# mLSTM: half of all heads' score weights made inside the projection, then the heads in pairs in the same block

## The chip, the cores and the metric

The kernel runs on one core of one Trainium2 chip. The metric is the device time of one execution in microseconds (us); where several runs are shown, their median.

## The reference, cut to what matters

One sequence of 256 tokens with 1024 features passes through three blocks of layers. The change touches one mixer of the third block, the mLSTM: 8 heads, queries and keys of 64, values of 128. Per head it computes, with `b` the running sum of the log forget gate and `li` the input gate:

```
qk = silu(causal_conv(proj[..., :2*M_QK]))
d  = where(mask, b[t] - b[s] + li[s], NEG)
m_t = maximum(inter, max(d))
s  = einsum(q, k) * exp(d - m_t)
den = sum(s)
h  = s @ v / maximum(abs(den), exp(-m_t))
out = (head_rmsnorm(h) * sigmoid(o)) @ w_out
```

The reference does this in chunks of 64 tokens with a carried state; the kernel does it for all 256 tokens at once, where no state is left.

## The kernel before, in words

The whole network is one program. A stage is a `nc.Block()`: inside it each engine runs its own list of instructions, in order, and at its end all engines meet. Weights stream from memory as chunks of 2 MB or 1.5 MB into a ring of four (`ring`); the queue of SyncE asks for the next as the tensor engine lets one go.

A product with exact float32 result is made of three products of rounded halves. The scalar engine writes the rounded part of a quarter of a chunk (`weights.high`, line 339, `weight_hi`), the vector engine the remainder (`weights.low`, line 346, `weight_lo`), and the tensor engine multiplies high by high, high by low and low by high (lines 516 to 518). A quarter of a chunk is called a part below. There are four places for parts. The scalar engine may write part b once the tensor engine has begun part b - 3, and the tensor engine may begin part b once the vector engine has done its remainder. So a part that is ready waits for up to three parts of tensor work.

The mLSTM mixer is `mlstm` (line 2589), in two stages:

- **Projection** (line 2600). Two chunks give queries and keys (parts 0 to 7), with one small product for the gates between them. Each block of 128 channels goes through the convolution on the vector engine (lines 2691, 2693) and Silu on the scalar engine (2665). Four more chunks give the values `v` (parts 8 to 15) and the output gate `out_gate` (parts 16 to 23). After the first of these the tensor engine turns the running sum into `decay` and repeats the key gates over all partitions (line 2635), and the scalar engine copies them to `key_gate` (2671). The vector engine copies each finished chunk product out of the banks (2708). At the end Sigmoid is applied to the whole `out_gate` (2675).
- **Heads** (line 2724). The loop at line 2737 takes one head after another. The lower triangle of 256 by 256 is kept as 384 columns: 128 for the first half of the queries ("near") and 256 for the second ("far"). Per head: the vector engine adds key gate, decay and mask (2773), takes the maximum of each row (2777) and turns it into a bias (2779, 2780); the scalar engine takes the exponential (2807); the vector engine multiplies by the scores of the tensor engine (2743, 2744) and sums (2788), makes the divisor (2792 to 2794) and scales the rows (2796); the tensor engine turns the three 128 by 128 pieces (2751), the scalar engine copies them to `weight_t` (2814), and the tensor engine multiplies by the values (2759 to 2761). `weight` and `weight_t` have two places each, and the order in which each engine goes through the steps of heads i, i-1 and i-2 is written out by hand.

The next stage is `add_gated`. It begins with the norm of each head (`HeadNorm`, line 2560 squares, 2568 sums, 2580 on GpSimd weighs the gate), turns the result (line 538) and multiplies it by `w_out`.

Of the kernel before, what the change touches and what calls it, by code (L numbers as in the profile page):

```python
# [22 lines left out]
ALU = mybir.AluOpType  # L23
ACT = mybir.ActivationFunctionType
# [347 lines left out]
def build(nc, d, widths, offsets):  # L372
    ctx = ExitStack()
    with ctx:
# [2214 lines left out]
        def mlstm(mem, x_parts, normalise):  # L2589
# [10 lines left out]
            with ExitStack() as conv, signals(  # L2600
                    "params_loaded", "t_ready", "t_read", "n_ready", "n_read", "dve_step", "pad_ready", "convolved", "o_copied",
                    "act_step", "summed", "turned", "pool_step", "pick_ready", "repeated", "repeated_read", *PARTS, *PreNorm.SIGNALS) as (
                    params_loaded, t_ready, t_read, n_ready, n_read, dve_step, pad_ready, convolved, o_copied,
                    act_step, summed, turned, pool_step, pick_ready, repeated, repeated_read, *sems):
                weights = weight_parts("t.tnnnn", sems[:len(PARTS)], conv)
                norm = normalise(x_parts, sems[len(PARTS):], conv, out_gate)
                raw = sbuf("raw", [P, DK, before + TOKENS], mem=conv)
                block = conv.enter_context(nc.Block())
# [31 lines left out]

                @block.scalar
                def _(act):
# [19 lines left out]
                    for b in range(DK):  # L2662
                        weights.high(act, DK + 4 + b // 3)
                        act.wait_ge(convolved, b + 1)
                        act.activation(qkT[:, b, :], qkT[:, b, :], ACT.Silu, bias=col("conv_b", b))
# [3 lines left out]
                    for n in range(HEADS_C // 2):  # L2669
                        act.wait_ge(repeated, n + 1)  # L2670
                        act.activation(key_gate[:, 2 * n:2 * n + 2, :], ps[:, (3, 0, 1, 3)[n], :].rearrange("p (b n) -> p b n", b=2),
                                       ACT.Copy).then_inc(repeated_read, 1)
                    weights.high(act, 24)
                    act.wait_ge(o_copied, 2)
                    act.activation(out_gate[:], out_gate[:], ACT.Sigmoid)

                @block.vector
                def _(dve):
# [25 lines left out]
                    for n in range(4):  # L2704
                        out = v if n < 2 else out_gate
                        weights.low(dve, DK + 4 * n + 7)
                        dve.wait_ge(n_ready, n + 1)
                        dve.tensor_copy(out[:, :, n % 2 * WIDE:n % 2 * WIDE + WIDE], bank_n(n)).then_inc(n_read, 1)
                        if n >= 2:
                            dve.wait_ge(n_read, n + 1)  # L2710
                            dve.memset(spare[:], 0.0).then_inc(o_copied, 1)
# [7 lines left out]

            with signals("scored", "biased", "exped", "probs_ready", "probs_turned", "turned_copied", "weighted", "dve_step") as (
                    scored, biased, exped, probs_ready, probs_turned, turned_copied, weighted, dve_step), ExitStack() as att:
                weight = sbuf("weight", [P, 2, TRI], mem=att)
                weight_t = sbuf("weight_t", [P, 2, TRI], mem=att)
                top = sbuf("top", [P, 2, TT], mem=att)
                least = sbuf("least", [P, 2, TT], mem=att)
                total = sbuf("total", [P, 2, TT], mem=att)
                part = (slice(0, P), slice(P, TRI))  # L2730
                keys = (P, TOKENS)
                n = HEADS_C
                block = att.enter_context(nc.Block())

                @block.tensor
                def _(pe):
                    for i in range(n + 2):
                        if i < n:
                            half = slice(i % 2 * HD, i % 2 * HD + HD)
                            if i >= 2:  # L2740
                                pe.wait_ge(probs_ready, i - 1)
                            q, k = qkT[half, i // 2, :], qkT[half, 4 + i // 2, :]
                            pe.matmul(ps[:, i % 2, 0:P], q[:, 0:P], k[:, 0:P], start=True, stop=True)
                            pe.matmul(ps[:, i % 2, P:TRI], q[:, P:TOKENS], k, start=True, stop=True).then_inc(scored, 1)
                        j = i - 1
                        if 0 <= j < n:
                            pe.wait_ge(probs_ready, j + 1)
                            if j >= 2:
                                pe.wait_ge(turned_copied, j - 1)
                            for b in range(3):  # L2750
                                last = pe.transpose(ps[:, 2 + j % 2, b * P:b * P + P], weight[:, j % 2, b * P:b * P + P], ident[:])
                            last.then_inc(probs_turned, 1)
                        j = i - 2
                        if j >= 0:
                            pe.wait_ge(turned_copied, j + 1)
                            t = weight_t[:, j % 2, :]
                            out = [ps[:, 4 + 2 * (j // 4) + a, j % 4 * P:j % 4 * P + P] for a in range(TT)]
                            val = [v[:, s, j * P:j * P + P] for s in range(TT)]
                            pe.matmul(out[0], t[:, 0:P], val[0], start=True, stop=True, skip_group_check=True)
# [827 lines left out]
```

## Time and profile before

| | |
|---|---|
| median of 3 runs | 3304.74 us (3301.76 to 3308.48) |
| profiled execution | 3303.2 us |
| its span, first to last instruction | 3301.5 us |
| mean granted clock of the tensor engine | 0.944 |
| tensor engine busy | 2961.6 us (90%) |
| vector engine busy | 2160.7 us (65%) |
| scalar engine busy | 1558.0 us (47%) |
| GpSimd busy | 104.1 us (3%) |

The tensor engine is busy in 90% of the span, but not evenly: the page's row of 40 slices has single slices at 5 tenths. The busy share of matmuls is of modelled ends, so a busy tensor engine isn't one at its peak. The granted clock is a share of full speed: 1.00 is 2.4 GHz, 0.50 is 1.2 GHz. Times in a timeline are from the start of the span.

### The profile page before, as it was taken

How to read it: one execution, taken by the hardware profiler on the slowest of the kernel's cores; microseconds unless marked ns; L12 is line 12 of the kernel's file. 1: busy time of each engine (PE TensorE's matmuls, PEld its weight loads, DVE VectorE, ACT ScalarE, POOL GpSimd, SP SyncE). 2: the span in 40 equal slices, each digit the busy share in tenths (PEclk: the TensorE clock that was granted, in tenths of full speed). 3: DMA queues.
4: the chain of work that ended last, by engine and by line, in shares of the span. 5: the costliest groups of instructions: out<-in, count | busy, mean ns of one | idle time of the engine just before them, and what ended most of it. 6: DMA issues, size and time to landing. Idle time of an engine off the chain costs nothing. (4 is left out here: it accounts for less than half of the span.)

```text
span 3301.5 us, 48307 instructions
## 1 busy us (share of the span) xinstructions
PE 2961.6 (90%) x19343; PEld 2611.4 (79%) x19343; DVE 2160.7 (65%) x3342; ACT 1558.0 (47%) x2451; POOL 104.1 (3%) x131
## 2 busy tenths in 40 slices
PE   7897998899999997778989799978997579999997
PEld 6896876579999997657977698758986569999996
DVE  5456598666666665276655665665555858888887
ACT  3442313444444444164443544534344248787875
POOL 0000000000000000200000000000000200000000
PEclk9998999999999998899998899969999879999999
DMA  6343498755666553304442254413553038888895
GB/s 270 145 179 139 160 369 344 307 198 203 217 209 223 193 199 142 124 26 153 178 163 106 102 181 151 167 50 134 191 188 113 0 150 334 338 332 325 330 336 189
DMA packets 76828, 648.61 MB, mean 196 GB/s; under 512 B 6105, under 2 KB 31193, under 8 KB 34033
## 3 DMA queue, kind: packets, MB, share of 16 engines
q1 hardware_dynamic: 49584, 621.09, 50.4%
q10 hardware_dynamic: 27072, 25.17, 2.3%
q8 instruction: 116, 1.90, 0.2%
q14 instruction: 56, 0.45, 0.0%
HBM read 632.60 MB, written 13.63 MB: 196 GB/s over the span
## 5 line engine op out<-in xcount | busy, mean ns | idle before, releaser
L1190 PE MATMUL ps<-x_hi,up_hi 128*128 128x256 f32 x1632 | 460.5, 282 | 3.7 <-DVE up_lo L1281 3.5
L346 DVE TENSOR_TENSOR weight_lo<-ring,weight_hi 128x1024 fp32r<-128x1024 f32 x236 | 288.4, 1235 | 263.5 <-ACT weight_hi L339 255.4
L1193 PE MATMUL ps<-x_lo,up_hi 128*128 128x256 f32 x1632 | 459.6, 282 | 0.0
L1194 PE MATMUL ps<-x_hi,up_lo 128*128 128x256 f32 x1632 | 459.5, 282 | 0.0
L339 ACT ACTIVATE weight_hi<-ring 128x1024 fp32r<-128x1024 f32 x236 | 245.7, 1054 | 190.6 <-PE ps L516 124.8
L1286 DVE TENSOR_TENSOR down_lo<-ring,down_hi 128x1024 fp32r<-128x1024 f32 x182 | 222.9, 1224 | 165.9 <-ACT down_hi L1243 165.9
L1190 PEld LDWEIGHTS ps<-x_hi,up_hi 128*128 128x128 f32 x1632 | 311.1, 191 | 11.8 <-DVE up_lo L1281 4.1
L1193 PEld LDWEIGHTS ps<-x_lo,up_hi 128*128 128x128 f32 x1632 | 311.1, 191 | 6.7
L1194 PEld LDWEIGHTS ps<-x_hi,up_lo 128*128 128x128 f32 x1632 | 311.1, 191 | 0.0
L1243 ACT ACTIVATE down_hi<-ring 128x1024 fp32r<-128x1024 f32 x182 | 193.2, 1062 | 232.1 <-PE ps L1215 232.1
L494 PE MATMUL ps<-x_hi,weight_hi 128*128 128x256 f32 x1024 | 291.5, 285 | 8.9 <-DVE weight_lo L346 8.1
L3283 DVE TENSOR_TENSOR up_lo<-ring,up_hi 128x1024 fp32r<-128x1024 f32 x242 | 294.4, 1217 | 4.2 <-ACT up_hi L3402 4.2
L495 PE MATMUL ps<-x_lo,weight_hi 128*128 128x256 f32 x1024 | 289.1, 282 | 0.0
L496 PE MATMUL ps<-x_hi,weight_lo 128*128 128x256 f32 x1024 | 288.9, 282 | 0.0
L3200 PE MATMUL ps<-up_hi,taken_hi 128*128 128x256 f32 x968 | 285.7, 295 | 2.1 <-DVE seat L3287 2.1
L1211 PE MATMUL ps<-down_lo,hidden_hi 128*128 128x512 f32 x728 | 285.7, 392 | 0.0
L1207 PE MATMUL ps<-down_hi,hidden_hi 128*128 128x512 f32 x728 | 284.1, 390 | 0.0
L3202 PE MATMUL ps<-up_hi,taken_lo 128*128 128x256 f32 x968 | 274.4, 283 | 0.0
L3201 PE MATMUL ps<-up_lo,taken_hi 128*128 128x256 f32 x968 | 274.2, 283 | 0.0
L3402 ACT ACTIVATE up_hi<-ring 128x1024 fp32r<-128x1024 f32 x242 | 256.1, 1060 | 32.5 <-PE ps L3202 25.0
L1281 DVE TENSOR_TENSOR up_lo<-ring,up_hi 128x1024 fp32r<-128x1024 f32 (+1 forms) x182 | 245.4, 1349 | 16.8 <-ACT up_hi L1237 16.8
L1215 PE MATMUL ps<-down_hi,hidden_lo 128*128 128x512 f32 x728 | 224.8, 390 | 0.0
(508 smaller groups left out, 6368.0 us busy)
## 6 DMA issues: line engine op xcount, KB each, us to landing
ring<-in_stream SPq DMA_DIRECT2D x181, 2048.0 KB, 7.8
ring<-in_experts SPq DMA_DIRECT2D x121, 1536.0 KB, 8.5
ring<-in_stream SPq DMA_DIRECT2D x22, 1536.0 KB, 6.4
gates<-kept_gates ACTq DMA_DIRECT2D x12, 1024.0 KB, 8.8
kept_gates<-away_first ACTq DMA_DIRECT2D x8, 768.0 KB, 10.6
kept_gates<-away_last ACTq DMA_DIRECT2D x8, 768.0 KB, 9.3
params_mix<-in_mix SPq DMA_DIRECT2D x1, 3072.0 KB, 21.9
params_ln<-in_ln SPq DMA_DIRECT2D x2, 1024.0 KB, 5.3
```

What stands on the lines that cost most here:

```text
L346: dve.tensor_tensor(self.place(self.lo, b), self.raw(b), self.place(self.hi, b), ALU.subtract).then_inc(self.split, 1)
L494: first = pe.matmul(out, hi[:, k, :], x_parts[0][:, k, :], start=(k == 0), stop=False)
L495: second = pe.matmul(out, hi[:, k, :], x_parts[1][:, k, :], start=False, stop=False)
L496: last = pe.matmul(out, lo[:, k, :], x_parts[0][:, k, :], start=False, stop=(k == DK - 1))
L1190: last = pe.matmul(out, hi[:, o:o + P], x_hi[:, k, :], start=(k == 0), stop=False)
L1193: pe.matmul(out, hi[:, o:o + P], x_lo[:, k, :], start=False, stop=False)
L1194: last = pe.matmul(out, lo[:, o:o + P], x_hi[:, k, :], start=False, stop=(k == DK - 1))
L1207: last = pe.matmul(out, hidden_hi[:, j % 2, tokens], hi[:, o:o + WIDE], start=(starts and i is None and j == 0), stop=False, skip_group_ch ...
L1211: pe.matmul(out, hidden_hi[:, j % 2, tokens], lo[:, o:o + WIDE], start=False, stop=False, skip_group_check=True)
L3200: pe.matmul(to, taken_hi[:, s % 3, k, :], hi, start=(k == 0), stop=False, skip_group_check=True)
L3202: last = pe.matmul(to, taken_lo[:, s % 3, k, :], hi, start=False, stop=(k == DK - 1), skip_group_check=True)
L3283: dve.tensor_tensor(up_part(up_lo, g, half), raw_up(g, half), up_part(up_hi, g, half), ALU.subtract).then_inc(up_split, 1)
```

## The change

The second stage of the mLSTM is gone; its work moves into the projection's stage.

- The vector engine makes the biased triangle, the row maxima and the biases of heads 0 to 3 between the remainders of parts 15 to 18, ahead of the copy of chunk product 1, and those of heads 4 to 7 between the remainders of parts 19 to 22, ahead of the copy of product 2. The steps on the maxima are made once for four heads.
- The scalar engine takes the exponentials of four heads after each of these, with parts 19 and 23 of the weights in between.
- All eight heads' triangles are kept, in the buffers `hT` (heads 0 to 4) and `raw` (heads 5 to 7), which are free by then; `weight_t`, `top`, `least` and `total` lie in the rest of `raw`.
- After the last projection matmul the heads go in pairs. The divisor is made once for two heads, and the scaling of the far columns moves from the vector engine to the scalar engine.
- The Sigmoid on `out_gate` is made in two halves, after the copies of pair 0 and of pair 1.

The diff, cut:

```diff
+                    def scores(p):
+                        for h in (2 * p, 2 * p + 1):
...
+                            pe.matmul(ps[:, h % 2, 0:P], q[:, 0:P], k[:, 0:P], start=True, stop=True)
+                            pe.matmul(ps[:, h % 2, P:TRI], q[:, P:TOKENS], k, start=True, stop=True).then_inc(scored, 1)
...
+                    pe.wait_ge(qk_ready, DK)
+                    pe.wait_ge(repeated_read, n_pairs)
+                    scores(0)
+                    pe.wait_ge(n_read, 4)
+                    for p in range(n_pairs):
+                        if p + 1 < n_pairs:
+                            pe.wait_ge(multiplied, p + 1)
+                            scores(p + 1)
+                        if p >= 1:
+                            values(p - 1)
+                        for h in (2 * p, 2 * p + 1):
+                            pe.wait_ge(near_ready, h + 1)
+                            pe.wait_ge(far_ready, h + 1)
+                            for b in range(3):
+                                last = pe.transpose(ps[:, 2 + h % 2, b * P:b * P + P], probs[h][:, b * P:b * P + P], ident[:])
+                            last.then_inc(probs_turned, 1)
+                    values(n_pairs - 1)
```

```diff
                 @block.scalar
+                    for g, heads in enumerate(halves):
+                        weights.high(act, DK + 11 + 4 * g)
+                        act.wait_ge(biased, g + 1)
+                        act.activation(least[:, heads[0]:heads[-1] + 1, :], top[:, heads[0]:heads[-1] + 1, :], ACT.Exp)
+                        for h in heads:
+                            for t in range(TT):
+                                o = probs[h][:, part[t]]
+                                last = act.activation(o, o, ACT.Exp, bias=top[:, h, t:t + 1])
+                            if h % 2 == 1:
+                                last.then_inc(exped, 1)
+                                weights.high(act, DK + 12 + 4 * g if h == heads[1] else 0)
                     weights.high(act, 24)
-                    act.wait_ge(o_copied, 2)
-                    act.activation(out_gate[:], out_gate[:], ACT.Sigmoid)
+                    for p in range(n_pairs):
+                        act.wait_ge(divided, p + 1)
+                        for h in (2 * p, 2 * p + 1):
+                            o = probs[h][:, part[1]]
+                            act.activation(o, o, ACT.Copy, scale=total[:, h, 1:2]).then_inc(far_ready, 1)
+                        for h in (2 * p, 2 * p + 1):
+                            act.wait_ge(probs_turned, h + 1)
...
+                            act.activation(weight_t[h % 2], ps[:, 2 + h % 2, 0:TRI], ACT.Copy).then_inc(turned_copied, 1)
+                        if p < TT:
+                            act.wait_ge(n_read, 4)
+                            act.activation(out_gate[:, p, :], out_gate[:, p, :], ACT.Sigmoid)
```

```diff
                 @block.vector
                     for n in range(4):
+                        if n in (1, 2):
+                            heads = halves[n - 1]
...
+                            dve.tensor_scalar(top[:, some, :], top[:, some, :], -1.0, None, ALU.mult).then_inc(biased, 1)
                         weights.low(dve, DK + 4 * n + 7)
                         dve.wait_ge(n_ready, n + 1)
                         dve.tensor_copy(out[:, :, n % 2 * WIDE:n % 2 * WIDE + WIDE], bank_n(n)).then_inc(n_read, 1)
-                        if n >= 2:
-                            dve.wait_ge(n_read, n + 1)
-                            dve.memset(spare[:], 0.0).then_inc(o_copied, 1)
+                    for p in range(n_pairs):
+                        dve.wait_ge(exped, p + 1)
+                        s = total[:, 2 * p:2 * p + 2, :]
+                        for h in (2 * p, 2 * p + 1):
+                            dve.wait_ge(scored, h + 1)
+                            for t in range(TT):
+                                o = probs[h][:, part[t]]
+                                last = dve.scalar_tensor_tensor(o, o, HD ** -0.5, ps[:, h % 2, part[t]], ALU.mult, ALU.mult,
+                                                                accum_out=total[:, h, t:t + 1])
+                        last.then_inc(multiplied, 1)
...
+                        dve.reciprocal(s, s).then_inc(divided, 1)
+                        dve.wait_ge(divided, p + 1)
+                        for h in (2 * p, 2 * p + 1):
+                            o = probs[h][:, part[0]]
+                            dve.tensor_scalar(o, o, total[:, h, 0:1], None, ALU.mult).then_inc(near_ready, 1)
```

The vector engine in the projection, before, from the copy of chunk product 0 to that of product 2:

```order
L2708 COPY v<-ps 128x2x512
L346 TENSOR_TENSOR weight_lo<-ring,weight_hi 128x1024 x4
L2708 COPY v<-ps 128x2x512
L346 TENSOR_TENSOR weight_lo<-ring,weight_hi 128x1024 x4
L2708 COPY out_gate<-ps 128x2x512
```

and with the change, from the copy of product 0 to that of product 1:

```order
L2802 COPY v<-ps 128x2x512
L346 TENSOR_TENSOR weight_lo<-ring,weight_hi 128x1024
L2789 SCALAR_TENSOR_TENSOR hT<-key_gate,decay,mask 128x128
L2789 SCALAR_TENSOR_TENSOR hT<-key_gate,decay,mask 128x256
...
L346 TENSOR_TENSOR weight_lo<-ring,weight_hi 128x1024
L2795 TENSOR_REDUCE raw<-hT 128x1 x8
L346 TENSOR_TENSOR weight_lo<-ring,weight_hi 128x1024
L2798 TENSOR_TENSOR raw<-raw,decay 128x8
L2799 TENSOR_SCALAR raw<-raw 128x8
L2802 COPY v<-ps 128x2x512
```

Where four remainders stood alone, eight additions (L2789), eight maxima and two small steps stand between them and ahead of the copy; the group between products 1 and 2 has the same form.

The scalar engine after the last exponential of the projection, with the change:

```order
L2742 ACTIVATE hT<-hT,raw 128x256 x2
L2747 ACTIVATE raw<-ps 128x384 x2
L2750 ACT_TABLE_LOAD
L2750 ACTIVATE out_gate<-out_gate 128x1024
L2742 ACTIVATE hT<-hT,raw 128x256 x2
L2747 ACTIVATE raw<-ps 128x384 x2
L2750 ACTIVATE out_gate<-out_gate 128x1024
```

L2742 is the scaling of the far columns, L2747 the copy of the turned pieces, L2750 the Sigmoid. Before, the Sigmoid stood ahead of the whole second stage; now its table load and first half stand between pair 0 and the far columns of pair 1, its second half between pairs 1 and 2.

The tensor engine, with the change, from the first scores to the turning of pair 1:

```order
L2662 MATMUL ps<-qkT 128x128
L2663 MATMUL ps<-qkT 128x256
...
L2690 MATMUL ps<-ident,hT 128x128 x6
L2662 MATMUL ps<-qkT 128x128
L2663 MATMUL ps<-qkT 128x256
L2662 MATMUL ps<-qkT 128x128
L2663 MATMUL ps<-qkT 128x256
L2671 MATMUL ps<-v,raw 128x128
L2672 MATMUL ps<-v,raw 128x128
L2673 MATMUL ps<-v,raw 128x128
...
L2690 MATMUL ps<-ident,hT 128x128 x6
```

L2662 and L2663 are scores, L2671 to L2673 values, L2690 turns a pair's six pieces. Two heads' scores now stand next to each other, and the scores of the next pair and the values of the pair before stand ahead of each turning.

## Rows read from the trace of the kernel before

**Rows 1.** Busy time of each engine by stretch: projection, change of stage, heads

```profile
core 0: us, PE busy (x) PEld busy (x) DVE busy (x) ACT busy (x) POOL busy (x), PEclk, DMA share, GB/s
2117.00:2156.00 39.00, 39.00 (x163) 31.32 (x162) 14.74 (x13) 13.40 (x15) 0.00 (x0) 0.96 0.37 140
2156.00:2160.00 4.00, 0.37 (x4) 0.11 (x2) 1.35 (x3) 2.03 (x2) 0.00 (x0) 0.81 0.00 0
2160.00:2190.00 30.00, 21.29 (x77) 15.51 (x77) 22.42 (x100) 10.37 (x28) 0.00 (x0) 0.50 0.00 1
```

**Rows 2.** Waits in the heads' stage: who waited for whom, us in total, times, longest

```profile
PE ps L2751 <- DVE weight L2796: 9.5, 7, 3.6
ACT least L2804 <- DVE top L2780: 9.4, 8, 1.3
```

**Rows 3.** Timeline of the vector engine, one head: start, us, engine, line, operation

```profile
2179.71 0.75 DVE L2773 SCALAR_TENSOR_TENSOR weight<-key_gate,decay,mask 128x128 f32<-128x128 f32 x2 [0.99 <-PE ps L2751]
2180.49 0.61 DVE L2777 TENSOR_REDUCE top<-weight 128x1 f32<-128x128 f32 x2
...
2181.42 0.29 DVE L2788 SCALAR_TENSOR_TENSOR weight<-weight,ps 128x128 f32<-128x128 f32 x1
...
2182.09 0.16 DVE L2792 SCALAR_TENSOR_TENSOR total<-total 128x2 f32<-128x2 f32 x1
...
2182.68 0.55 DVE L2796 TENSOR_SCALAR weight<-weight,total 128x128 f32<-128x128 f32 x2
```

**Rows 4.** Timeline of the scalar engine: a table load, the Sigmoid, one head

```profile
2105.15 1.28 ACT L2661 ACT_TABLE_LOAD   x1
2106.45 0.42 ACT L2661 ACTIVATE gate_t<-gate_t 8x256 f32<-8x256 f32 x1
...
2157.72 1.91 ACT L2675 ACTIVATE out_gate<-out_gate 128x2048 f32<-128x2048 f32 x1 [9.98 <-DVE spare L2711]
...
2181.65 0.78 ACT L2807 ACTIVATE weight<-weight,top 128x128 f32<-128x128 f32 x2
...
2184.23 0.49 ACT L2814 ACTIVATE weight_t<-ps 128x384 f32<-128x384 f32 x1 [1.80 <-PE ps L2751]
```

**Rows 5.** Timeline of the tensor engine: last projection matmul, heads 0 and 1, head 5, the end

```profile
2155.90 0.39 PE L518 MATMUL ps<-weight_hi,x_lo 128*128 128x512 f32 x1
...
2159.92 0.81 PE L2743 MATMUL ps<-qkT 64*128 64x128 f32 x4 [3.63 <-PEq L2600]
2160.48 1.10 PE L2744 MATMUL ps<-qkT 64*128 64x256 f32 x4
...
2183.29 0.91 PE L2751 MATMUL ps<-ident,weight 128*128 128x128 f32 x3 [0.76 <-DVE weight L2796]
2183.99 0.64 PE L2759 MATMUL ps<-v,weight_t 128*128 128x128 f32 x2
...
2185.41 0.79 PE L2743 MATMUL ps<-qkT 64*128 64x128 f32 x2
...
2196.57 0.39 PE L2761 MATMUL ps<-v,weight_t 128*128 128x128 f32 x2
```

**Rows 6.** Timeline of the vector engine: copies of chunk products, the last remainder

```profile
2133.94 1.23 DVE L2708 COPY v<-ps 128x1024 f32<-128x1024 f32 x1 [0.25 <-PE ps L518]
...
2146.46 1.23 DVE L346 TENSOR_TENSOR weight_lo<-ring,weight_hi 128x1024 fp32r<-128x1024 f32 x1
...
2156.33 1.23 DVE L2708 COPY out_gate<-ps 128x1024 f32<-128x1024 f32 x1 [8.64 <-PE ps L518]
```

**Rows 7.** The scalar engine's roundings in the projection's last 39 us, with mean ns

```profile
L339 ACT ACTIVATE weight_hi<-ring 128x1024 fp32r<-128x1024 f32 x9 | 9.6, 1061 | 15.3 <-PE ps L516 15.2
```

**Rows 8.** Busy time by stretch in another mixer's heads (columns as in rows 1)

```profile
1434.80:1458.80 24.00, 19.52 (x162) 12.32 (x164) 23.25 (x52) 19.47 (x68) 0.00 (x0) 1.00 0.00 1
1462.20:1469.00 6.80, 3.76 (x32) 2.52 (x34) 3.36 (x10) 4.06 (x11) 0.00 (x0) 1.00 0.02 4
```

**Rows 9.** The tensor engine's transposes there

```profile
L1070 PE MATMUL ps<-ident,prob 128*128 128x128 f32 x48 | 7.0, 282 | 4.9 <-DVE prob L1094 4.9
```

More of the change, by code:

```diff
@@ L2607, in mlstm @@
                 raw = sbuf("raw", [P, DK, before + TOKENS], mem=conv)
+                hT_flat = hT[:].rearrange("p k n -> p (k n)")
+                raw_flat = raw[:].rearrange("p k n -> p (k n)")
+                in_hT = DK * TOKENS // TRI
+                probs = [hT_flat[:, h * TRI:h * TRI + TRI] if h < in_hT else raw_flat[:, (h - in_hT) * TRI:(h - in_hT) * TRI + TRI]
+                         for h in range(HEADS_C)]
+                raw_rest = raw_flat[:, (HEADS_C - in_hT) * TRI:]
+                weight_t = [raw_rest[:, b * TRI:b * TRI + TRI] for b in range(2)]
+                top, least, total = (raw_rest[:, 2 * TRI + b * HEADS_C * TT:2 * TRI + (b + 1) * HEADS_C * TT].rearrange("p (h t) -> p h t", t=TT)
+                                     for b in range(3))
+                part = (slice(0, P), slice(P, TRI))
+                keys = (P, TOKENS)
+                halves = (range(0, HEADS_C // 2), range(HEADS_C // 2, HEADS_C))
+                n_pairs = HEADS_C // 2
                 block = conv.enter_context(nc.Block())
@@ L2664, in _ @@
                         act.wait_ge(convolved, b + 1)
-                        act.activation(qkT[:, b, :], qkT[:, b, :], ACT.Silu, bias=col("conv_b", b))
+                        act.activation(qkT[:, b, :], qkT[:, b, :], ACT.Silu, bias=col("conv_b", b)).then_inc(qk_ready, 1)
                     weights.high(act, DK + 7)
@@ L2705, in _ @@
                         out = v if n < 2 else out_gate
+                        if n in (1, 2):
+                            heads = halves[n - 1]
+                            some = slice(heads[0], heads[-1] + 1)
+                            for h in heads:
+                                if h % 2 == 0:
+                                    weights.low(dve, DK + 4 * n + 4 + h % 4 // 2)
+                                    dve.wait_ge(repeated_read, h // 2 + 1)
+                                for t in range(TT):
+                                    last = dve.scalar_tensor_tensor(probs[h][:, part[t]], key_gate[:, h, 0:keys[t]], decay[:, t, h:h + 1],
+                                                                    mask[:, part[t]], ALU.add, ALU.add)
+                            weights.low(dve, DK + 4 * n + 6)
+                            step(last)
+                            for h in heads:
+                                for t in range(TT):
+                                    last = dve.tensor_reduce(top[:, h, t:t + 1], probs[h][:, part[t]], AX.X, ALU.max)
+                            weights.low(dve, DK + 4 * n + 7)
+                            step(last)
+                            step(dve.tensor_tensor(top[:, some, :], top[:, some, :], decay[:, :, some].rearrange("p t h -> p h t"), ALU.max))
+                            dve.tensor_scalar(top[:, some, :], top[:, some, :], -1.0, None, ALU.mult).then_inc(biased, 1)
                         weights.low(dve, DK + 4 * n + 7)
```

118 lines of the change are left out of this document (26 added, 92 removed).

## The prediction

> **What bounds the kernel now.** I read busy time by stretch first [rows 1]. In the projection the tensor engine (PE) never stops, at clock 0.96, while the vector engine (DVE) is busy 14.7 of 39 us and the scalar engine (ACT) 13.4. In the heads no engine is full: over 30 us PE has 21.3, DVE 22.4, ACT 10.4, and the clock is 0.50, its lower level of 1.2 GHz. Memory is quiet (1 GB/s). The waits [rows 2] are a ring: PE's turning waits for DVE's scaling and ACT for DVE's bias; and DVE's next triangle waits for that turning, 0.99 us at 2179.71 [rows 3]. One head's turn of the ring is 2179.71 to 2184.23, where the next turning frees ACT [rows 3, 4], 4.52 us. So the heads are bound by a chain through three engines, not by anyone's work. The stretch that can change runs from the last projection matmul (issued 2155.90, done 2156.3) to the last value matmul (2196.57 + 0.39 = 2196.96) [rows 5]: 40.7 us. In it lie the copy of the last product, the Sigmoid of 1.91 us [rows 4, 6], the change of stage (PE next starts at 2159.92) and eight heads.
>
> **What moves into the projection.** Per head DVE adds (two additions, 0.75 us, of which 0.08 overlaps what follows: 0.67) and takes maxima (0.61, so 0.54) [rows 3]. A group of four heads costs 2.7 + 2.2, and the small steps, made once, 0.6: 5.5 us. The group's own work is four remainders of 1.23 (1.15 back to back) and a copy of 1.23 [rows 6], about 6.1. That is 11.6 us for four parts that PE works through in 11.2: the copies of products 1 and 3 stand at 2133.94 and 2156.33, eight parts apart, so a part is 2.8 us [rows 6]. DVE falls behind by 0.4 us a group and lives on its lead. ACT gets 0.78 (0.7 back to back) per head of exponentials [rows 4], 3.0 us a group with the small one, and a table load that falls into a wait; with four roundings of 1.06 [rows 7] it has 7.2 of 11.2 us.
>
> The tight place is the end. Rounding of part 18 ends near 2132.4 as now; maxima, remainder 18 and small steps take DVE to 2134.8; exponentials of heads 0 and 1 (1.5) and rounding 19 (1.06) take ACT to 2137.4. From there DVE has four remainders, eight additions, eight maxima and the small steps in one row: 4 x 1.15 + 2.7 + 2.2 + 0.5 = 10.0, bias ready at 2147.4. ACT: two heads' exponentials 1.5, rounding 23 1.06, to 2150.0; remainder 23 done at 2151.2. PE wants part 23 at 2156.1 - 2.8 = 2153.3. The lead there falls from 5.6 us (2146.46 + 1.23 = 2147.7 now [rows 6]) to 2.1 and is not used up. Cost: 0. If the added operations cost half as much again (2.8 us a group), part 23 would be some 3 us late.
>
> **What is left behind it.** At the full clock, times on before's axis:
> - Copy of the last product 2156.33 to 2157.6 [rows 6]. Pair 0's scores run under it: two heads' scores took 2159.92 to 2161.58 at the low clock, no longer than one head's (2185.41, 0.79 and then 1.06), since they use different halves of the rows [rows 5]; so 0.8 us a pair at full clock.
> - Products and sums: 2182.09 - 2181.42 = 0.67 a head, 1.3 a pair: 2158.9. Divisor 0.6 [rows 3]: far scaling can start at 2159.6. From 2156.3 that is **3.3 us**.
> - ACT from there is the slowest of the three: two far scalings (0.4 each, the copy of 384 columns being 0.49), two copies 0.9 after a wait of 0.3 for the turning, table load 1.28, half a Sigmoid 1.0 [rows 4]. Pair 1's far scaling waits behind all of it, until 2163.85: **4.25**. PE would need only 0.8 + 1.3 + 0.65 = 2.75 a pair (a head's values are half of 2185.41 - 2183.99 less a gap of 0.14, 0.64; its turning half of 2183.99 - 2183.29, 0.33 [rows 5]), DVE 2.4.
> - Pair 1's scalings, turning, copies and the other half Sigmoid, 0.8 + 0.3 + 0.9 + 1.0: **3.0**, to 2166.85.
> - Pair 2: scaling to first turning 0.5, turning 0.75, copy 0.4, two value products 1.3; pair 3: turning 0.65 (its scaling is ready), copy 0.45, two value products and their tail 1.5: **5.55**, to 2172.4.
>
> Sum 16.1 us against 40.7: 24.6 less. The next stage is unchanged: the same instructions start it after the same meeting of the engines, and no weight transfer is in flight in the heads to be missed [rows 1].
>
> **One rule weighed.** The table load at 2105.15 took 1.28 us and the activation after it started at 2106.45, 0.02 us behind its end [rows 4]. The Trainium skill, ScalarE: Activation LUTs, "What ACT_TABLE_LOAD costs", adds a drain of about 1.38 us to the 1283 ns, which speaks against a Sigmoid inside the loop. By it pair 1 would come 1.4 us later and the gain be 23.2. The trace disagrees about the drain, so the sum keeps 1.28.
>
> **The clock** is the open term. It fell at about 2158.5 (0.81 over 2156 to 2160 [rows 1]), after 2.2 us without a matmul. With the change PE rests at nearly the same place, from 2157 to 2159. Another mixer's heads, with waits between them, kept 1.00 while PE was busy 19.5 of 24 us, and then 3.76 of 6.8 [rows 8]. Bounds: it never falls (24.6), or it falls at 2158.5 and never returns. Then PE is the bound at 1.45 for a pair's scores, 2.56 values, 1.3 turning: four turnings 5.2, four value pairs 10.2, three scores 4.35, waits 0.7, tail 0.25, from 2159.05 to 2179.8, a gain of 17.2. I take the near end, since after 2159 PE is busier than in [rows 8], less 1.1 us for a low stretch or for waits that the walk takes too short: **23.5**. The profiled execution's 3303.2 less 23.5 is 3279.7; the median is 1.5 above that execution, so 3281.2, rounded 3281.
>
> **Rivals.**
> - *Low clock all through the pairs.* For it: the fall at 2158.5, and 0.50 in 30 us of today's heads. Against it: those have a head's 4.52 us with gaps, the pairs have almost none. Time 3304.7 - 17.2 = 3287.5. The Trainium skill, TensorE: Matmul & The Clock Gate, "Part 4: PE-mode transpose", says that the full clock does not engage for transposes, which would help this rival; the 48 transposes at line 1070 lie in a stretch at 1.00 [rows 8, 9], so there they did not take it away. Chance 0.18.
> - *The splits come late.* ACT and DVE work strictly in order, so whatever the added operations take beyond the rows holds back rounding or remainder. At half as much again PE loses 3 us in the projection, at twice as much 9: 3284 to 3290. For it: DVE's 11.6 against 11.2. Against it: 2.1 us of lead, and the same forms are in [rows 3]. Chance 0.08.
> - *Slower than before.* The same lateness, but so early that PE stands ahead of part 15 and the clock falls and stays low for parts 15 to 23: at half the clock a part of 2.8 us [rows 6] takes up to 5.6, so 9 x 2.8 = 25.2, with 5 us of standing and only the 17.2 of the cold pairs: 13.0 slower, 3317.7. It decides only if lateness recurs at every part; a single fall recovers, as after the gates' product (projection at 0.96 [rows 1]). Chance 0.02.
> - *The change doesn't do what it says* (a hidden wait keeps the heads in sequence). Eight triangles have eight places, so the one wait of DVE on the turning is gone. A gain of only the stage change and the moved work would be about 13 us: 3292. Chance 0.03.
>
> **How the numbers follow.** Forecast 0.69, the rivals 0.18, 0.08, 0.02 and 0.03. Range: below, a gain of 24.6 and the 3 us by which the fastest run lies under the median, 3277; above, the cold rival 3287.5 and 1.5 for scatter, 3289. This leaves out the slower rival, the last one and part of the lateness. A measurement of this kernel tells 0.2%, 6.6 us, from no change; every case but the slower one gains more. Faster 0.96, same 0.02, slower 0.02.
>
> **What would show it.** Right: no wait of PE for `weight_lo` between parts 15 and 23; last value matmul some 16 us after the last projection matmul; PE waiting once, about 1 us, for pair 1's far scaling behind the table load and Sigmoid; granted clock near 1.00 in the pairs. Wrong step by step: gaps of PE in the projection (lateness), clock 0.50 after the copy and PE without gaps for 20 us (low clock), DVE's two additions of a head longer than 0.75 us in `hT` and `raw`. The forecast as a whole is wrong if the stretch is longer than 21 us.

## The result and the profile after

The changed kernel took **3280.82 us** (median of 4 runs, 3279.23 to 3284.80) against 3304.58 us for the kernel before beside it (4 runs): ratio 0.993, 95% interval 0.9918 to 0.9943. Measured again beside three variants it took 3281.82 us against 3304.86 (0.9932, 0.9918 to 0.9945). The forecast was 3281.0.

| | before | after |
|---|---|---|
| profiled execution / its span | 3303.2 / 3301.5 us | 3282.36 / 3280.6 us |
| mean granted clock | 0.944 | 0.947 |
| last projection matmul ends | 2156.29 | 2159.41 |
| last value matmul ends | 2196.96 | 2176.11 |
| between them (the **stretch**) | 40.67 us | 16.70 us |
| from there to the next stage's turning (L538) | 10.78 us | 11.55 us |

"The stretch" is meant in this sense from here on. Busy time by stretch, after, for [rows 1]:

```profile
core 0: us, PE busy (x) PEld busy (x) DVE busy (x) ACT busy (x) POOL busy (x), PEclk, DMA share, GB/s
2117.00:2156.00 39.00, 39.00 (x159) 31.20 (x158) 25.94 (x50) 20.01 (x35) 0.00 (x0) 0.91 0.41 148
2156.00:2160.00 4.00, 4.00 (x23) 2.97 (x21) 0.56 (x1) 0.00 (x0) 0.00 (x0) 1.00 0.00 0
```

The projection took up the work without a gap: DVE rises from 14.7 to 25.9 us of 39 and ACT from 13.4 to 20.0, and PE is busy in all 39. The list of PE's waits has none for `weight_lo` there. Then the pairs, where [rows 1] had 30 us at clock 0.50:

```profile
2160.00:2165.00 5.00, 3.12 (x24) 2.09 (x22) 4.70 (x27) 2.03 (x5) 0.00 (x0) 0.85 0.01 2
2165.00:2170.00 5.00, 5.00 (x36) 3.76 (x33) 2.78 (x18) 4.69 (x7) 0.00 (x0) 0.81 0.01 3
2170.00:2175.00 5.00, 4.50 (x38) 4.02 (x37) 1.81 (x11) 3.48 (x9) 0.00 (x0) 1.00 0.00 2
```

The clock fell here too, at 2163.5 (4.1 us behind the last projection matmul's end), but for 3.4 us only; before it fell at 2158.5 for 37.5 us. The prediction had it near 1.00 in the pairs. DVE around the end of the projection, for [rows 3, 6]:

```profile
2144.22 1.40 DVE L2789 SCALAR_TENSOR_TENSOR raw<-key_gate,decay,mask 128x128 f32<-128x128 f32 x4
...
2150.16 1.22 DVE L2802 COPY out_gate<-ps 128x1024 f32<-128x1024 f32 x1
2152.87 1.23 DVE L346 TENSOR_TENSOR weight_lo<-ring,weight_hi 128x1024 fp32r<-128x1024 f32 x1 [1.49 <-ACT weight_hi L339]
2159.44 1.22 DVE L2802 COPY out_gate<-ps 128x1024 f32<-128x1024 f32 x1 [5.35 <-PE ps L518]
2160.58 0.28 DVE L2810 SCALAR_TENSOR_TENSOR hT<-hT,ps 128x128 f32<-128x128 f32 x1
```

The additions of two heads take 1.40 us, twice the 0.67 of a head back to back and the 0.08 of overlap: what [rows 3] had. The last remainder ends at 2154.10, and PE begins part 23 at 2156.49 (its twelve products start 0.23 us apart and end at 2159.41): a lead of 2.4 us. ACT in the pairs, for [rows 4]:

```profile
2162.43 0.91 ACT L2742 ACTIVATE hT<-hT,raw 128x256 f32<-128x256 f32 x2 [8.21 <-DVE raw L2816]
2163.64 0.49 ACT L2747 ACTIVATE raw<-ps 128x384 f32<-128x384 f32 x1 [0.30 <-PE ps L2690]
2164.36 0.49 ACT L2747 ACTIVATE raw<-ps 128x384 f32<-128x384 f32 x1 [0.23 <-PE ps L2690]
2164.87 1.28 ACT L2750 ACT_TABLE_LOAD   x1
2166.16 1.06 ACT L2750 ACTIVATE out_gate<-out_gate 128x1024 f32<-128x1024 f32 x1
2167.12 0.89 ACT L2742 ACTIVATE hT<-hT,raw 128x256 f32<-128x256 f32 x2
...
2170.05 0.50 ACT L2742 ACTIVATE hT<-hT,raw 128x256 f32<-128x256 f32 x1
```

These rows carry the walk of the prediction: pair 0's far scaling at 2162.43, pair 1's at 2167.12, pair 2's at 2170.05. The activation behind the table load starts 0.01 us after its end. And PE, for [rows 5]:

```profile
2159.66 0.61 PE L2663 MATMUL ps<-qkT 64*128 64x256 f32 x4
2161.93 0.50 PE L2662 MATMUL ps<-qkT 64*128 64x128 f32 x4 [1.67 <-DVE hT L2810]
...
2163.08 1.24 PE L2690 MATMUL ps<-ident,hT 128*128 128x128 f32 x6 [0.21 <-ACT hT L2742]
2164.25 0.81 PE L2662 MATMUL ps<-qkT 64*128 64x128 f32 x4
...
2167.79 0.89 PE L2690 MATMUL ps<-ident,hT 128*128 128x128 f32 x6
...
2175.72 0.39 PE L2673 MATMUL ps<-v,raw 128*128 128x128 f32 x2
```

Pair 0's scores run under the copy of the last product. PE waits 1.67 us for DVE to free the scores' banks; pair 1's turning at 2167.79 has no wait.

Of the profiled spans' 20.9 us, the stretch gives 24.0. Given back are 2.1 in stages ahead of the mLSTM's gates (they are unchanged: scatter between executions), 1.0 in the projection (a low-clock stretch of 6.8 us from 2122.6 instead of 3.4) and 0.8 in the head norm, with 0.8 the other way behind it. The second profiled execution of the same kernel had a span of 3277.3 and a stretch of 17.34, so of single executions 2 or 3 us are scatter.

The two executions differ in where the low 3.4 us lie. In the second the clock fell 2.7 us behind the last projection matmul (2158.01, with the projection done at 2155.33), so that they cover pair 1's scores, pair 0's turning and only the beginning of pair 2's scores:

```profile
2159.35 1.54 PE L2690 MATMUL ps<-ident,hT 128*128 128x128 f32 x6
...
2164.33 0.92 PE L2690 MATMUL ps<-ident,hT 128*128 128x128 f32 x6 [0.77 <-DVE hT L2820]
```

From pair 0's to pair 1's far scaling it takes 5.34 us there (2158.35 to 2163.69) and 4.69 in the first. Other runs below with the same pairs agree: 4.68 us with the fall 4.1 us behind the projection (maxima twice), 5.39 and 5.25 with the fall ahead of pair 0's turning (two blocks; weighing on DVE). So the place of the low stretch is worth about 0.65 us, and where the clock fell has to be looked up before two profiles are compared.

### The profile page after: what moved, and what is told of

It is laid out like the page before. It is cut to its first block and busy times, and to the rows that moved or that the text cites. A ratio compares the mean times of both kernels' runs of the same rounds, so it can differ in the third digit from the quotient of the medians.

```text
span 3280.6 us, 48259 instructions
## 1 busy us (share of the span) xinstructions
PE 2953.2 (90%) x19343; PEld 2606.9 (79%) x19343; DVE 2152.5 (66%) x3308; ACT 1558.9 (48%) x2454; POOL 103.0 (3%) x131
```

## The experiments

My theory: three things add up, the work moved into the projection, the pairs, and the single block; the clock is a consequence. Rivals: that one of the three does all of it, or that the clock does. First each part was undone.

**The work not moved.** Same block, same pairs; the additions, maxima, biases and exponentials of all heads stand behind the last product's copy.

```diff
 for n in range(4):
-    if n in (1, 2):
-        heads = halves[n - 1]
...
     dve.tensor_copy(out[:, :, n % 2 * WIDE:n % 2 * WIDE + WIDE], bank_n(n)).then_inc(n_read, 1)
+for n in (1, 2):
+    heads = halves[n - 1]
...
 for p in range(n_pairs):
     dve.wait_ge(exped, p + 1)
```

> The pairs and the one stage stay; additions, maxima, biases and exponentials of all heads come after the copy of the last product instead of inside the projection. Theory (the moved work was on the path): the vector engine puts 2 x 5.5 us between that copy and the first product, so the stretch from the last projection matmul to the last value matmul is 16.7 + 11.0 = 27.7 us, up to 31 if the clock falls in the longer rest, and about 3292 us in all. Rival (the heads were bound by the ring of waits, the moved work was hidden beside it anyway): 17 to 19 us and about 3282. In both the projection of the tensor engine is unchanged.

Measured 3295.73 us (ratio 0.9974, 0.9963 to 0.9986), stretch 28.63. The clock was low from 2164.4 to 2178.0, 13.7 us, most of them PE's wait for this work.

```profile
2158.38 1.23 DVE L2781 COPY out_gate<-ps 128x1024 f32<-128x1024 f32 x1 [8.44 <-PE ps L518]
2159.52 2.71 DVE L2789 SCALAR_TENSOR_TENSOR hT<-key_gate,decay,mask 128x128 f32<-128x128 f32 x8
2162.27 2.17 DVE L2794 TENSOR_REDUCE raw<-hT 128x1 f32<-128x128 f32 x8
...
2169.91 0.17 DVE L2797 TENSOR_SCALAR raw<-raw 128x8 f32<-128x8 f32 x1
```

From 2159.52 to 2170.1 DVE makes what it otherwise makes beside the projection. The move is worth 28.63 - 16.70 = 11.9 us of the stretch, 11.0 of them foreseen as DVE's work.

**Heads one by one.** Moved work and single block stay; scores, scaling, turning and values go head by head.

```diff
-for p in range(n_pairs):
-    if p + 1 < n_pairs:
-        pe.wait_ge(multiplied, p + 1)
-        scores(p + 1)
+for h in range(HEADS_C):
+    if h + 1 < HEADS_C:
+        if h >= 1:
+            pe.wait_ge(multiplied, h)
+        scores(h + 1)
...
```

> As the change, but scores, products, divisor, scaling, turning and values go head by head, each engine in its own order. Theory (pairs matter, since two heads' scores take the time of one and the divisor's three small steps are made once for two): tensor engine 0.8 + 0.64 + 0.33 = 1.8 us a head instead of 2.75 a pair, so 3 to 5 us more than the 16.7 of the change: 20 to 22, about 3285 us in all. Rival (only the move into the projection and the single stage matter): 16.7 within 1 us, about 3281.

Measured 3296.70 us (0.998, 0.997 to 0.9989), stretch 32.31: 15.6 over the pairs, far more than either theory gave it.

```profile
2160.00:2190.00 30.00, 27.57 (x96) 20.25 (x97) 11.19 (x65) 10.48 (x19) 0.00 (x0) 0.53 0.00 1
```

PE was busy 27.57 of 30 us. The clock fell at 2162.0 and stayed at its lower level for 44 us: the 29 us left of the heads, in which PE hardly rested, and 15 behind them. So the clock was not a mere consequence of waits, and two experiments had to part it from the pairs' other merits.

**One by one, with filler.** Three products of 128x128 more per head (from the second on, 21 in all), into a place written over later.

```diff
 values(h - 1)
+for _ in range(3):
+    pe.matmul(ps[:, 6, 3 * P:4 * P], weight_t[(h - 1) % 2][:, 0:P], v[:, 0, (h - 1) * P:h * P],
+              start=True, stop=True, skip_group_check=True)
```

> As the run with the heads one by one, with three more value products of 128x128 per head, made again into a place that is written over later. The question is how much of that run's 15.6 us over the pairs was the clock, which fell at 2162.0 and stayed at its lower level for 44 us while PE was busy 27.7 of 30 us. If the fillers bring the full clock back, a head costs PE 1.9 + 0.8 us and the chain about 3, so the stretch from the last projection matmul to the last value matmul is 25 to 28 us (32.3 without fillers): more work in less time, about 3291. Rival, the clock doesn't depend on such work and stays low: 8 heads of 3.8 + 1.5 us, stretch 42 to 46 us, about 3308.

Measured 3293.68 us (0.9961, 0.9947 to 0.9975), stretch 27.90: more work, 4.4 us less time.

```profile
2162.00:2170.00 8.00, 7.31 (x29) 5.70 (x30) 3.17 (x19) 2.70 (x5) 0.00 (x0) 0.57 0.01 2
2170.00:2187.00 17.00, 15.04 (x110) 12.41 (x109) 6.91 (x40) 7.78 (x15) 0.00 (x0) 1.00 0.00 0
```

The clock came back after 6.8 us. Turnings of successive heads, first without and then with filler, show the price of the clock:

```profile
2169.96 0.88 PE L2690 MATMUL ps<-ident,hT 128*128 128x128 f32 x3 [0.28 <-ACT hT L2741]
...
2173.78 0.85 PE L2690 MATMUL ps<-ident,hT 128*128 128x128 f32 x3
```

```profile
2174.15 0.83 PE L2688 MATMUL ps<-v,raw 128*128 128x128 f32 x6
2174.82 0.49 PE L2693 MATMUL ps<-ident,hT 128*128 128x128 f32 x3
...
2177.54 0.49 PE L2693 MATMUL ps<-ident,hT 128*128 128x128 f32 x3
```

A head takes 3.82 us at the low clock, and 2.72 at the full one of which 0.67 is filler: 2.05. Over some seven heads that is 12 us, an estimate from above of the clock's share of the 15.6: at the full clock and without filler another engine may set the pace of a head, and no run shows that case. The clock did come back with this filler in the heads.

**Scores in pairs, the rest one by one.** Against the run with the heads one by one:

```diff
-if h + 1 < HEADS_C:
-    if h >= 1:
-        pe.wait_ge(multiplied, h)
-    scores(h + 1)
+if h % 2 == 1 and h + 1 < HEADS_C:
+    pe.wait_ge(multiplied, h + 1)
+    scores((h + 1) // 2)
```

> Scores made for two heads at once, everything behind them head by head. It takes from the run with the heads one by one only the double cost of the scores: 1.65 us per head at the low clock against 1.66 per pair. If the clock stays low as there, 8 x 0.83 = 6.6 us less: stretch 25.7 us, about 3290. If the paired scores are what lets the clock return (theory: two heads on different halves of the rows keep PE fuller), the stretch is 17 to 20 us and the time 3281 to 3284, so that hardly anything of the pairs' gain would be their fewer waits.

Measured 3290.27 us (0.9955, 0.9939 to 0.9972), stretch 26.63. The clock was low from 2163.8 for 17.1 us, then full. The first theory's 25.7 was near, the second's 17 to 20 fell: the clock came back late, not at once. The 5.7 us saved (6.6 expected) aren't the scores' own work alone: the last 6.7 us ran at the full clock, and PE now waits where it didn't before (2.25 and 1.21 us for ACT's scaling). The run doesn't part these. PE was busy 14.4 of the 17 low us, a smaller share than with the heads one by one, and yet the clock returned.

**A stage of their own.** The change, with the pairs in a second block.

```diff
     for n in range(1, 4):
         parts_n(pe, weights, x_parts, n, n_ready, n_read)
+stage.close()
+block = conv.enter_context(nc.Block())
+@block.tensor
+def _(pe):
     def scores(p):
```

> The change, but with the pairs in a stage of their own behind the projection, as the heads were before. Pair 0's scores then stand behind the copy of the last product and the meeting of the engines. Before, PE began 2.3 us after that copy's end and its scores took 0.8: 3.0 us later than in the changed kernel, stretch 19.7 us, time about 3284. Rival: the longer rest (about 4.5 us without a matmul) makes the clock fall before the pairs begin and stay low in them: stretch 25 us or more, time 3289 or more.

Measured 3286.74 us (0.9942, 0.9925 to 0.9959), stretch 18.97, 2.3 more than in the first profile of the changed kernel; the clock was low for 3.4 us. From the last projection matmul to pair 0's far scaling it takes 4.59 us instead of 3.02, so 1.6 us are the block's own (3.0 expected). The other 0.7 lies in the next step (5.39 instead of 4.69): the clock fell ahead of pair 0's turning, as in the changed kernel's second profile (5.34).

**Maxima made twice, and three times.** How much lateness does the projection bear?

```diff
+tensor_reduce(total[:, h, t:t + 1], probs[h][:, part[t]], AX.X, ALU.max)
 tensor_reduce(top[:, h, t:t + 1], probs[h][:, part[t]], AX.X, ALU.max)
```

> The eight maxima of each group are made twice (first into a place that is overwritten later), 2.2 us more of the vector engine in each group. Theory (the lead at the last parts is about 2.3 us and is what covers the moved work): the tensor engine stands some 2.3 us in all ahead of parts 22 and 23, nowhere else, and the time grows by 2 to 3 us. Rival (the projection has room for much more, the scalar engine's waits show it): no standing, time unchanged.

> The maxima of each group are made three times, 4.4 us more of DVE per group than in the changed kernel. With one repetition (2.2 us more) PE stood 1.1 us ahead of part 23 and the stretch did not change. Theory, the lead at the end was 2.3 us at part 23 and everything beyond it is paid once: PE stands 3 to 4 us in parts 20 to 23, and the time is 3 to 4 us above the changed kernel, about 3284. Rival (what the prediction held possible): lateness recurs at parts 15 to 19 too and the clock falls in the projection: PE stands over 6 us, granted clock under 0.9 between parts 15 and 23, time over 3290.

Twice: 3280.02 us (0.9933, 0.9916 to 0.9949), stretch 16.65. Three times: 3285.37 us (0.994, 0.9923 to 0.9956), stretch 16.86. PE ahead of part 23 with the maxima made twice:

```profile
2154.59 0.50 PE L516 MATMUL ps<-weight_hi,x_hi 128*128 128x512 f32 x1 [1.10 <-DVE weight_lo L346]
```

and ahead of parts 19 and 22 with the maxima made three times:

```profile
2146.26 0.51 PE L516 MATMUL ps<-weight_hi,x_hi 128*128 128x512 f32 x1 [0.40 <-DVE weight_lo L346]
...
2158.54 0.79 PE L516 MATMUL ps<-weight_hi,x_hi 128*128 128x512 f32 x1 [3.74 <-DVE weight_lo L346]
```

The lead of 2.4 us is used up by 2.2 us more per group, with 1.10 over: 1.2 us of the first group's lateness are carried into the second (counted back from the projection's end, less PE's standing, remainder 19 comes 1.2 us later than in the changed kernel and remainder 23 3.3). The time doesn't show the 1.10: 3280.02 beside 3280.82 for the changed kernel, where the theory had 2 to 3 us more. With 4.4 more PE stands 4.1 us in all, 0.40 of them ahead of part 19: at this size lateness does come at the end of the first group too, and the expectation of standing in parts 20 to 23 alone missed that. The clock fell within the projection only after the long standing (2156.7, for 6.8 us, all of part 22). The time is 4.6 us above the changed kernel's, 3 to 4 expected.

**The Sigmoid ahead of the pairs,** so that it doesn't stand between pair 0 and pair 1.

```diff
 weights.high(act, 24)
+for n in (2, 3):
+    act.wait_ge(n_read, n + 1)
+    half = out_gate[:, :, n % 2 * WIDE:n % 2 * WIDE + WIDE]
+    act.activation(half, half, ACT.Sigmoid)
 for p in range(n_pairs):
...
-    if p < TT:
-        act.wait_ge(n_read, 4)
-        act.activation(out_gate[:, p, :], out_gate[:, p, :], ACT.Sigmoid)
```

> The Sigmoid of the first half of the columns follows the last exponential, that of the second half the last product's copy, both ahead of pair 0; its table load falls into the scalar engine's rest before the last copy. Theory (the scalar engine's order costs something in the pairs only where the clock is full): 16.7 us become 15.0 to 16.7, 0 to 1.5 us less in all. Rival (the second half's Sigmoid, 1 us, now lies between the copy and pair 0's scaling): the first turning 0.2 us or more later, nothing gained.

Measured 3283.60 us (0.9938, 0.9922 to 0.9955), stretch 16.31. That is 0.4 us less than in the first profile of the changed kernel. But here the clock fell 2.6 us behind the last projection matmul, which is where it fell in the second profile (2.7), and that one had 17.34. Like for like the move saves 1.0 us, within the theory's 0 to 1.5; from pair 0's to pair 1's far scaling it takes 3.01 us instead of 5.34, and 1.3 us of this are lost again behind it. The comparison rests on one profile each, and the medians (3283.60 and 3280.82) tell no gain.

**The gate's weighing moved off GpSimd's start of the head norm.** The trace after showed a wait that I had not looked at. Before and after:

```profile
2197.26 1.94 ACT L2560 ACTIVATE square<-ps 128x1024 f32<-128x1024 f32 x2 [1.57 <-PEq L2724]
2197.75 4.52 POOL L2580 TENSOR_TENSOR out_gate<-out_gate,params_mlstm 128x2048 f32<-128x2048 f32 x1 [126.28 <-POOLq L2724]
...
2200.69 1.61 DVE L2570 TENSOR_SCALAR head_var<-head_var 128x16 f32<-128x16 f32 x1
```

```profile
2176.41 1.94 ACT L2560 ACTIVATE square<-ps 128x1024 f32<-128x1024 f32 x2 [1.58 <-PEq L2600]
...
2177.68 4.51 POOL L2580 TENSOR_TENSOR out_gate<-out_gate,params_mlstm 128x2048 f32<-128x2048 f32 x1 [103.77 <-issue]
...
2179.84 2.38 DVE L2570 TENSOR_SCALAR head_var<-head_var 128x16 f32<-128x16 f32 x1
```

DVE's operation on 16 columns takes 1.61 and 2.38 us: it ends when GpSimd's multiplication ends, and that starts 0.49 us behind ACT's squares before and 1.27 behind them after. Two variants take the multiplication away from there: one gives it to DVE behind its last scaling (the diff), one makes it on GpSimd in two halves, each behind its half of the Sigmoid. The changed kernel ran again beside them.

```diff
 dve.tensor_scalar(o, o, total[:, h, 0:1], None, ALU.mult)
+dve.wait_ge(gated, TT)
+dve.tensor_tensor(out_gate[:], out_gate[:], spread(p_norm_w, 1, TT), ALU.mult)
```

> The changed kernel, with the gate's multiplication by norm_w (GpSimd, 4.51 us from 2177.68, at the start of the head norm) made by DVE behind its last scaling of the pairs, where DVE is idle for 5.5 us. In the changed kernel DVE's small operation L2570 ends only with that multiplication (2182.22), GpSimd's power follows at 2182.30 and takes 2.91 us, and DVE's last product of the norm waits 0.73 us for it. Theory: with GpSimd free the small operation takes 0.2 us instead of 2.38, the power ends at about 2182.9 and the last product starts there or behind the two products (2182.3) at about 2182.9: the time from the last value matmul to the next stage's turning falls from 11.55 to 9.2 us, 2.3 us less, about 3278.5. Rival: the multiplication on DVE (2.35 us) ends behind the last value matmul and holds up the meeting of the engines, then nothing is gained.

> As weighed_dve, but the multiplication stays on GpSimd and is made in two halves within the pairs, with both Sigmoid halves ahead of pair 0. The head norm gains the same 2.3 us. Theory: DVE's scalings stand still while GpSimd multiplies, as L2570 did (2.38 us for 128x16), so each half of 2.25 us can hold back one pair, and the stretch grows by up to 2 us against the run with the early Sigmoid (16.3): about 3281, the gain given back. Rival: the two don't meet and the stretch stays 16.3: 3278.5.

> The changed kernel itself, unchanged, beside the three variants on the same chip: about 3281 us and a ratio of 0.993 to before, as in its first measurement.

On DVE: 3278.81 us (0.9923, 0.9909 to 0.9936), against 3281.82 for the changed kernel beside it. On GpSimd: 3281.12 us (0.9927, 0.9913 to 0.994), stretch 19.29. The first half runs at 2157.78, beside the projection's last part, and meets nothing; only the second lies in the pairs. The last value matmul to the next turning takes 9.35 us in both.

```profile
2179.22 0.18 DVE L2571 TENSOR_SCALAR head_var<-head_var 128x16 f32<-128x16 f32 x1
2179.31 2.35 DVE L2575 TENSOR_TENSOR v<-ps,out_gate 128x1024 f32<-128x1024 f32 x2
2179.49 2.91 POOL L2586 TENSOR_TENSOR head_var<-head_var,minus_half 128x16 f32<-128x16 f32 x1 [105.16 <-DVE head_var L2571]
```

0.18 us in place of 2.38. With the second half on GpSimd within the pairs the stop comes there (pair 0's divisor, 4 columns):

```profile
2162.86 0.16 DVE L2818 SCALAR_TENSOR_TENSOR raw<-raw 128x4 f32<-128x4 f32 x1
2163.05 2.20 DVE L2819 TENSOR_TENSOR raw<-raw 128x4 f32<-128x4 f32 x1
```

```profile
2162.87 2.36 POOL L2836 TENSOR_TENSOR out_gate<-out_gate,params_mlstm 128x1024 f32<-128x1024 f32 x1 [2.69 <-ACT out_gate L2744]
```

GpSimd ends at 2165.23, DVE's 4 columns at 2165.25. The theory of the gain given back held, with more given back than its 2 us: the stretch is 3.0 us longer than with the early Sigmoid (16.31). Of these 2.0 lie ahead of pair 0's far scaling, and from 2164.2 on the clock was low for 6.8 us instead of 3.4.

**Weighing on DVE, with filler where PE waits for pair 0.**

```diff
 scores(0)
 pe.wait_ge(n_read, 4)
+for _ in range(10):
+    pe.matmul(ps[:, 6, 3 * P:4 * P], qkT[:, 0, 0:P], v[:, 0, 0:P], start=True, stop=True, skip_group_check=True)
```

> As weighed_dve, and PE makes ten products of 128x128 that nobody reads (1.1 us at the full clock) while it waits for pair 0's multiplication, behind pair 0's scores. In the changed kernel it waits 1.67 us there and the clock falls at 2163.3 for 3.4 us. If PE's rest is what lets it fall, it stays at its upper level in the pairs and the stretch falls by 0.5 to 1.5 us (16.7 to about 15.7), about 3277.5. Rival: the clock falls all the same, then the stretch stays 16.7 or gets longer by what the products take.

Measured 3278.94 us (0.9921, 0.9908 to 0.9935), stretch 17.32 (17.26 without filler, in this pair of profiles). Each product is two instructions here, so the ten took 2.4 us and not 1.1, and held back pair 1's scores and pair 0's turning. The clock, though, stayed at 1.00 from the projection to the last value:

```profile
2160.00:2165.00 5.00, 4.54 (x33) 3.58 (x33) 3.23 (x14) 0.38 (x1) 0.00 (x0) 1.00 0.01 2
2165.00:2170.00 5.00, 4.47 (x38) 3.33 (x36) 3.57 (x23) 3.71 (x7) 0.00 (x0) 1.00 0.01 3
2170.00:2176.00 6.00, 5.25 (x43) 4.38 (x43) 4.26 (x19) 5.11 (x12) 0.00 (x0) 1.00 0.00 0
```

And yet nothing is gained, since two things cancel between the far scalings of pairs 0 and 1 (5.31 us with filler, 5.25 without). Pair 0's turning begins 1.58 us behind its far scaling with filler (2164.62 to 2166.20) and 0.90 without: 0.7 lost. From there to pair 1's far scaling it takes 3.73 us at the full clock (to 2169.93) and 4.35 without filler, where the clock was low from 2161.0 to 2164.4: 0.6 won. Behind pair 1's far scaling the clock was full in both, and it takes 8.98 us to the last value in both. The rival came true for the time (the stretch stayed), not for the clock. A filler that ends before pair 0's multiplication does is not tested. The version with the weighing on DVE has the lowest median of all; its interval overlaps that of the changed kernel, so that it is faster rests on the 2.2 us of the trace.

## Why the prediction was right

Its steps, measured between the same events:

| step | foreseen | after | second execution |
|---|---|---|---|
| last projection matmul to pair 0's far scaling | 3.3 | 3.02 | 3.02 |
| to pair 1's far scaling (ACT's row) | 4.25 | 4.69 | 5.34 |
| to pair 2's far scaling | 3.0 | 2.93 | 2.93 |
| to the last value matmul | 5.55 | 6.06 | 6.05 |
| sum | 16.1 | 16.70 | 17.34 |

- **Projection at no cost.** Right, with the lead of 2.1 us measured as 2.4. The doubled maxima stand for the lateness rival: its mechanism exists and begins where the forecast put it, at part 23. The 3 us it gave for "half as much again" (2.8 us a group) were too many: 1.1 and 4.1 us were measured for 2.2 and 4.4 more, and a straight line between them gives 1.9, an estimate. It carried the first group's lateness on in full. The slower rival needed lateness at every part; even the tripled maxima gave 0.40 us at part 19 and 3.74 at part 22, and low clock for 6.8 us.
- **The walk.** ACT's row between the pairs is longer than foreseen in both executions. In the first, half of the excess of 0.44 is a second wait of ACT for a turning (0.23), where the walk had one of 0.3. In the second the turning ran at the low clock and ACT waited 1.03 us for it. The last step's 0.51 is ACT's copies: each waits 0.5 to 0.85 for a turning and PE then 0.25 for the copy, a ring that the walk priced lower.
- **The table load.** No drain behind it, 2164.87 + 1.28 to 2166.16, as in [rows 4]. So the trace disagrees a second time with the Trainium skill, ScalarE: Activation LUTs, "What ACT_TABLE_LOAD costs", on this.
- **PE's wait of about 1 us at pair 1** depends on the clock. In the first execution it did not appear: PE worked at the low clock just then (pair 2's scores 1.66 instead of 0.8, the first head's values 1.28 instead of 0.67) and reached the turning as ACT had the scaling ready, so the slack paid for the clock. In the second, with the clock full again by then, it is there with 0.77 us (2164.33). The row names DVE, whose scaling was long done (2161.76); ACT's far scaling began at 2163.69. The run in two blocks (0.82) and the one with the weighing on DVE (0.69) have it too.
- **The clock.** The sign "near 1.00 in the pairs" was wrong: the rows show 0.85 and 0.81. The 1.1 us set aside for a low stretch or for waits covered what came: 0.6 in the first execution, 1.24 in the second, of which 0.65 is the low stretch lying on pair 0's turning. The chance of 0.18 for "low clock all through" had a real mechanism, and it is near: with single heads it happens, to their end. The argument against it, that pairs leave PE few gaps, was too simple. The single heads leave few gaps too (27.57 of 30 us busy), and there the clock stayed low. That pairs differ by more than their gaps was right by luck.
- **The next stage unchanged.** Same instructions, but 0.77 us longer, since GpSimd's start slipped from 0.49 to 1.27 us behind ACT's. All runs that leave the weighing there show 11.55 to 11.57, the one in two blocks too; what delays GpSimd stays open.

That 3281.0 and 3280.82 differ by only 0.2 us is luck as well: the range of the four runs is 5.6 us.

The parts, undone singly, are worth 11.9 (move), 15.6 (pairs, up to 12 of them the clock) and 2.3 us (block, 1.6 of them its own) of the stretch. They add to 29.8 and not 24.0. That each removes waits which another would also remove is my reading; no run undoes two of them at once.

## What to carry to other kernels

Before pricing a loop of small matmuls at the full clock, ask what the order of the work does to the clock: here a head's products, one head after another, cost 3.82 us at the low clock and 2.05 (an estimate) at the full one, and it showed in no list of waits, since PE was busy all along. Then ask where the low stretch lies: 3.4 us of it cost 0.65 us more on the path to ACT's copies than beside ACT's own work. In this kernel work moved into another engine's stage was free up to the lead at the last part, and the lead is read from the trace in one subtraction. Where a stage begins, look for a long GpSimd instruction beside a tiny one of the vector engine.

## What the runs showed of the hardware

- With heads one by one PE was busy 27.57 of 30 us and the clock stayed at its lower level (1.2 GHz) to their end and 15 us beyond, 44 us in all; with 21 more 128x128 products it was back at 1.00 after 6.8 us. In pairs it returned after 3.4 us (after 6.8 where GpSimd held up pair 0), with scores alone in pairs after 17.1, in which PE was busy 14.4 of 17 us. So the busy share in these rows doesn't tell the cases apart, and what in the single heads keeps the clock low (their 64-row scores, turnings or short gaps) the runs don't part.
- Two heads' scores on different halves of the rows take 1.66 us at the low clock (2164.25 to 2165.91), one head's took 1.65.
- A vector operation on 4 or 16 columns takes 2.20 and 2.38 us beside a GpSimd multiplication, and 0.16 and 0.18 without; it ends with GpSimd's. The reductions beside it are not held (2.35 us for two, with or without). The Trainium skill, SBUF — State Buffer, "Who interferes with whom", describes an exclusive lock held for a whole instruction, from which reductions are free; the trace agrees.
